# First expert stage: the gates of two prompt tiles added into DRAM by GpSimd's indirect DMAs instead of one-hot products

## The reference

```python
sc, ci = lax.top_k(cand, PEER_TOPK)
eid = (take_along_axis(i1, ci // PEER_TOPK, -1) * N_KEYS + take_along_axis(i2, ci % PEER_TOPK, -1))
gate = jax.nn.softmax(sc, -1)
hid = jax.nn.gelu(einsum('td,thkd->thk', xt, expert_u[eid]))
return einsum('thk,thkd->td', gate * hid, expert_v[eid])
```

## Time and profile before

| | us |
|---|---|
| median of 3 runs | 2101.57 (2098.19 to 2106.11) |
| the profiled execution | 2104.75 |
| its span, first to last instruction | 2103.0 |

### The profile page before, as it was taken

The page is one execution under the profiler, slowest core; times in us unless marked ns, Lnnn a source line. Parts: engine busy times, 40 slices in busy tenths (PEclk is TensorE's granted clock), DMA queues, the critical chain, the costliest instruction groups (busy, mean ns, idle before and its releaser), DMA issues.

```text
span 2103.0 us, 33945 instructions
## 1 busy us (share of the span) xinstructions
PE 2018.1 (96%) x12943; PEld 1851.9 (88%) x12943; DVE 1619.7 (77%) x3030; ACT 794.4 (38%) x1311; POOL 542.5 (26%) x334
## 2 busy tenths in 40 slices
PE   8999889889999899999999999999989999999998
PEld 8998879778866899999999999999978888888886
DVE  6735766565254325999999799999969999999997
ACT  4335453342241322232244344444434333333332
POOL 0000020000000000212111045555537656666530
PEclk9999989989999999999999999999999999999999
DMA  5224210061451402677676579999999999999992
GB/s 172 81 89 129 81 52 1 22 225 41 166 197 62 160 1 89 222 279 247 225 245 237 184 238 334 330 333 333 334 375 396 411 412 411 411 411 411 407 353 93
DMA packets 205520, 483.75 MB, mean 230 GB/s; under 512 B 11983, under 2 KB 104655, under 8 KB 205286
## 3 DMA queue, kind: packets, MB, share of 16 engines
q1 hardware_dynamic: 159334, 314.56, 41.3%
q0 software_dynamic: 46080, 167.79, 21.7%
HBM read 423.29 MB, written 58.36 MB: 229 GB/s over the span
## 4 chain that ended last, share of the span: by engine, by line
PE 58%; DMA 1%; SPq 1%; ACT 0%; DVE 0%; issue 0%; POOL 0%; DVEq 0%
PE ps L3001 24%; PE ps L2609 8%; PE ps L2605 8%; PE ps L2604 8%; PE ps L2595 5%; PE ps L2633 4%; DMA outputs<-peer_v,kept 1%; SPq L2563 0%; SPq L2586 0%; DMA experts<-peer_u 0%; ACT scores L2690 0%; DMA hidden<-kept 0%; PE ps L3027 0%; PE ps L3032 0%; ACT kept L2679 0%
## 5 line engine op out<-in xcount | busy, mean ns | idle before, releaser
L3001 PE MATMUL ps<-v_high_low,gated_high_low 128*128 128x512 f32 x2304 | 526.1, 390 | 8.2 <-ACT gated_high_low L3069 7.4
L3001 PEld LDWEIGHTS ps<-v_high_low,gated_high_low 128*128 128x128 f32 x2304 | 434.0, 189 | 100.1 <-ACT v_high_low L3067 7.7
L2604 PE MATMUL ps<-x_high_low,u_high_low 128*128 128x384 f32 x1024 | 355.6, 347 | 0.2 <-ACT u_high_low L2670 0.2
L2605 PE MATMUL ps<-x_high_low,u_high_low 128*128 128x384 f32 x1024 | 345.0, 337 | 0.0
L3093 POOL DMA_INDIRECT outputs<-peer_v,kept x138 | 255.8, 1854 | 155.7 <-DVE kept L3110 121.5
L2721 POOL DMA_INDIRECT scores<-peer_u,kept x64 | 95.1, 1485 | 733.5 <-DVE kept L2841 556.9
L2679 ACT ACTIVATE kept<-ps 128x384 f32<-128x384 f32 x128 | 62.9, 491 | 407.5 <-PE ps L2609 404.3
L2609 PE MATMUL ps<-x_high_low,u_high_low 128*128 128x384 f32 x1024 | 204.7, 341 | 0.0
L2604 PEld LDWEIGHTS ps<-x_high_low,u_high_low 128*128 128x128 f32 x1024 | 192.5, 188 | 0.5 <-ACT u_high_low L2670 0.5
L2605 PEld LDWEIGHTS ps<-x_high_low,u_high_low 128*128 128x128 f32 x1024 | 192.8, 188 | 0.0
L3110 DVE SCALAR_TENSOR_TENSOR kept<-outputs,kept 128x1024 f32<-128x1024 f32 x136 | 174.3, 1281 | 8.9 <-DMA outputs<-peer_v,kept 5.5
(11 more groups left out here) (471 smaller groups left out, 4136.7 us busy)
## 6 DMA issues: line engine op xcount, KB each, us to landing
experts<-peer_u SPq DMA_DIRECT2D x63, 1024.0 KB
raw_v<-peer_v SPq DMA_DIRECT2D x60, 1024.0 KB
hidden<-kept SPq DMA_DIRECT2D x64, 384.0 KB, 3.5
gates<-scores SPq DMA_DIRECT2D x12, 2048.0 KB
first_hidden<-hidden SPq DMA_DIRECT2D x16, 768.0 KB, 10.4
outputs<-gates SPq DMA_DIRECT2D x16, 768.0 KB
outputs<-hidden SPq DMA_DIRECT2D x16, 768.0 KB
first_gates<-gates SPq DMA_DIRECT2D x15, 768.0 KB
```

Of the source, the lines that this page charges most:

```text
L2604: pe.matmul(o, utr[:, b, HI, k], xr[:, HI, k, 0:DN], start=(k == 0), stop=False)
L2605: pe.matmul(o, utr[:, b, HI, k], xr[:, LO, k, 0:DN], start=False, stop=False)
L3001: ins = pe.matmul(bank(c, 2 * t + h), gr[:, slot, x, DN * b + P * t:DN * b + P * t + P], vr[:, slot, y, D * b + 512 * h:D * b + 512 * h + ...
```

## The change

For tiles 0 and 1 (`SCATTERED`) the gates matrix isn't made by products. Instead:

- POOL sets a tile of 128 x 1024 zeros, ACT waits for it and issues eight DMAs of 2 MB each from it (`ZEROS`), which zero the two thirds of `gates_dram` that belong to tiles 0 and 1. This is the first thing that ACT does in the stage.
- Tile 0 is picked first, then 4, 3, 1, 2. After the picks of tiles 0 and 1 DVE computes the cells of their 128 pairs (`place`, seven small operations), runs as many `low`s as bring it to a given group (`caught_up`), and divides the gates (`divided`), for which ACT has to reach `EXPS_AT`, group 7 for tile 0 and group 31 for tile 1.
- POOL issues 128 accumulating indirect DMAs for each of the two tiles (`scatter`): each adds one number per token, 128 numbers of 4 bytes, into DRAM. After every 16 of them it waits until those before have landed (the 16 pairs of one head have different cells, those of two heads may not).
- The 160 gathers are put between the scatters by fixed counts: none ahead of the 64th scatter of tile 0, 18 by the end of tile 0, 19 more behind it, 96 among the scatters of tile 1, and the last 27 after them.
- Tile 2 keeps the one-hot products: 16 octets in place of 48, in the last 32 steps, four tokens in each; `QT` goes from 2 to 4, `BEFORE` from 39 to 47. Behind the last pick two dots stand after each low (`IN_GAP`).

```diff
-GATES_AT = 25
+EXPS_AT = {0: 7, 1: 31}
-DOTS_BY = {4: 0, GT: 16, 0: 32, 1: 46, 2: 59}
+DOTS_BY = {0: 0, 4: 0, GT: 16, 1: 32, 2: 46}
+ZEROS = 8
+IN_GAP = 2
+GATHERED = [18, 37]
...
+            act.wait_ge(zeros_set, 1)
+            for i in range(ZEROS):
+                g = slice(NG // ZEROS * i, NG // ZEROS * (i + 1))
+                act.dma_start(gates_by_group(c)[:, g, 0:FIRST_G].rearrange("p n g x -> p n (g x)"), over(zeros, 1, [P, NG // ZEROS, FIRST_G * GB * TG])).then_inc(zeroed, 16)
             keep(0, 0)
...
+            def scatter(n, j):
+
+                if j and j % TOPK == 0:
+                    pool.wait_ge(scattered[n], 16 * j)
+                pool.indirect_dma_start(out=gates_flat(c), out_offset=bass.IndirectOffsetOnAxis(ap=cells[n][:, j:j + 1], axis=0),
+                                        in_=gates_of[n][:, j:j + 1], in_offset=None, compute_op=ALU.add).then_inc(scattered[n], 16)
+
+            pool.memset(zeros, 0.0).then_inc(zeros_set, 1)
+            pool.wait_ge(zeroed, 16 * ZEROS)
+            pool.wait_ge(cells_set, 1)
+            for j in range(PAIRS):
+                scatter(0, j)
+                if j >= PAIRS // 2:
+                    gather(GATHERED[0] * (j + 1 - PAIRS // 2) * 2 // PAIRS)
+            gather(GATHERED[1])
+            pool.wait_ge(cells_set, 2)
+            for j in range(PAIRS):
+                scatter(1, j)
+                gather(GATHERED[1] + (PAIRS * 3 // 4) * (j + 1) // PAIRS)
+            gather(ROWSETS)
...
             while lows[0] < UG * BEFORE:
                 low()
+                for _ in range(IN_GAP):
+                    dot()
```

More of the change, by code:

```diff
@@ L71 @@
 K_SEL = _cols(SAMP)
+K_PLACE = _cols(8)
 K_N = _at
@@ L2390 @@
 NTG = DN // TG
+SCATTERED = (0, 1)
+HOTS = [n for n in range(DENSE) if n not in SCATTERED]
+HG = len(HOTS) * (P // TG)
+FIRST_G = NTG - HG
+HC = P * len(HOTS)
 UG = 2
@@ L2487, in phase_hidden @@
     places = words(c, H_B + 512, 2, PAIRS)
-    kept, kt = words(c, H_K, NT, 3, 128), words(c, H_T, 4, DN)
-    gate, inv = words(c, H_V, DN), words(c, H_V + DN, DN)
+    kept, kt = words(c, H_K, NT, 3, 128), words(c, H_T, 4, HC)
+    gate, inv = words(c, H_V, HC), words(c, H_V + HC, HC)
     firm = plain(c.hot[:, :])
     hot2, gated = [firm[:, 0:OCT * P], firm[:, 2 * OCT * P:3 * OCT * P]], [firm[:, OCT * P:2 * OCT * P], words(c, H_HOT, OCT * P)]
+    zeros, cells = firm[:, 0:(NTG - HG) * GB * TG], {n: kept[:, n, 0].bitcast(U32) for n in SCATTERED}
     gst = [words(c, a, NK, TG) for a in F_GST]
@@ L2834, in divided, with place, caught_up @@
                 return v.tensor_tensor(g3, g3, over(head_sum, 2, [P, PH, TOPK]), ALU.mult)
+            def place(n):
+                step(v.tensor_copy(hi, kept[:, n, 0]))
+                step(v.tensor_scalar(hi, hi, 2, None, ALU.logical_shift_right))
+                v.tensor_copy(hif, hi)
+                step(v.scalar_tensor_tensor(lof, kept[:, n, 1], float(NG * NTG * GB), kept[:, n, 0], ALU.mult, ALU.add))
+                step(v.scalar_tensor_tensor(lof, hif, float((NTG - 1) * GB), lof, ALU.mult, ALU.add))
+                step(v.tensor_scalar(lof, lof, float(TG), cst(c, K_PLACE + n, 1), ALU.mult, ALU.add))
+                step(v.tensor_copy(cells[n], lof))
+            def caught_up(q):
+                while lows[0] < UG * q + 1:
+                    low()
+            pick(0, DOTS_BY[0]).then_inc(picked, 1)
+            v.wait_ge(picked, 1)
+            place(0)
+            caught_up(EXPS_AT[0])
+            divided(0, 0).then_inc(cells_set, 1)
             pick(4, DOTS_BY[4]).then_inc(picked, 1)
-            v.wait_ge(picked, 1)
+            v.wait_ge(picked, 2)
             step(v.scalar_tensor_tensor(eid, kept[:, 4, 0], float(NK), kept[:, 4, 1], ALU.mult, ALU.add))
@@ L2844, in _ @@
             pick(GT, DOTS_BY[GT]).then_inc(picked, 1)
-            v.wait_ge(picked, 2)
+            v.wait_ge(picked, 3)
             step(v.scalar_tensor_tensor(tail, kept[:, GT, 0], float(NK), kept[:, GT, 1], ALU.mult, ALU.add))
             v.tensor_copy(ids[:, PAIRS_EACH:], tail).then_inc(ids_set, 1)
-            for n in range(3):
-                pick(n, DOTS_BY[n]).then_inc(picked, 1)
-                v.wait_ge(picked, n + 3)
-                if n == 1:
-                    while lows[0] < UG * GATES_AT + 1 and lows[0] < UG * BEFORE - 1:
-                        low()
-                    step(divided(4, 0))
-                    step(divided(GT, 1))
+            pick(1, DOTS_BY[1]).then_inc(picked, 1)
+            v.wait_ge(picked, 4)
+            place(1)
+            caught_up(EXPS_AT[1])
+            step(divided(4, 1))
+            step(divided(GT, 2))
+            divided(1, 3).then_inc(cells_set, 1)
+            pick(2, DOTS_BY[2]).then_inc(picked, 1)
             while lows[0] < UG * BEFORE:
                 low()
+                for _ in range(IN_GAP):
+                    dot()
             v.wait_ge(sums, 1)
-            step(v.reciprocal(inv, bank(c, 6, DN)))
+            step(v.reciprocal(inv, bank(c, 6, HC)))
             v.tensor_tensor(kt[:, 3], gate, inv, ALU.mult).then_inc(gates_set, 1)
@@ L2863, in _ @@
             low()
-            before, octets = dots[0], NTG * QG // 2 + 3
-            for o in range(NTG * QG // 2):
+            before, octets = dots[0], HG * QG // 2 + 3
+            v.wait_ge(zeroed, 16 * ZEROS)
+            for o in range(HG * QG // 2):
                 t0, slot = OCT * o, o % 2
@@ L2874, in _ @@
                 v.tensor_tensor(k1, k1, over(kt[:, 3, t0:t0 + OCT], 2, [P, OCT, NK]), ALU.mult).then_inc(hot_set, 1)
-                if lows[0] < NK:
-                    low()
+                for _ in range(QT * UG * 2 // QG):
+                    if lows[0] < NK:
+                        low()
                 while dots[0] < min(ROWSETS, before - (before - ROWSETS) * (o + 1) // octets):
```

81 lines of the change are left out of this document (48 added, 33 removed).

## The result

The change makes the kernel slower: 2392.8 us median of 4 runs (2388.2 to 2395.6) against 2100.5 for the kernel before in the same runs. The ratio is 1.1385, 95% interval [1.1354, 1.1415]. The forecast was 2245 us with a range of 2080 to 2400: the place and the kind of the loss were right, its size was half of what came. The profiled execution took 2390.97 us; that is +286 on the 2104.75 of before.

The account below looks back on a forecast made before the run. PE was taken to bound the stage, with DVE in lockstep and nearly full. Saved products -57.6, start +27 and DVE's waits for POOL +44, +44, +87 gave +144 us: 2249 profiled, 2245 us median, range 2080 to 2400.

Parts of the forecast that it names:

- Products, -57.6: One-hot gate products on PE: removing 256 at 0.225 us saves 57.6 us, all of it on the path.
- The start, +27: Stage start: ACT's eight zeroing DMAs fill the queue and delay its first copies and PE by 27 us.
- The scatter's price, 1.24 us: POOL's queue: one scatter takes 1.24 us from start to start, like a gather; bounds 0.30 and 2.28 us.
- 229x - 140.5: Whole change in us, if one scatter costs POOL x us from start to start; turns to a loss at x = 0.61.
- A: DVE's first dot: waits 44 us for the first gathered row behind POOL's scatters.
- B: The fifteen dots after the first: POOL needs 100 us against PE's 56, another 44 us lost.
- C: After the last pick, gap and octets: POOL needs 311 us against PE's 224, 87 us lost.
- The 27 gathers after that are hidden: Stage end: the last 27 gathers take at most 62 us beside PE's last 70, so cost nothing.
- The picks of tile 1 and 2, nothing lost: Picks of tiles 1 and 2: no scatters stand ahead of what they need, so no time is lost.
- Dearer scatters: Rival: scatters cost more than gathers, in POOL or DMA engines; 2.28 us each gives about 2485 us; chance 0.17.
- likeliest case: POOL sets the stage's pace about as worked out, 2180 to 2330 us; chance 0.50.
- Cheap: Rival: scatters cost POOL little, 0.5 us each, making the kernel faster at 2083 or 2059 us; chance 0.15.

Follow-up runs that it names:

- hots-first run: Changed kernel without scatters, zeroing spread, fewer dots left for the end, each octet's two lows behind the one-hots with two dots between: 2087.6 us, 0.9931.
- both tiles, paced: Changed kernel with zeroing spread, lows apart behind the one-hots, dots redistributed, 8 scatters and then 1.8 after each gather: 2319.3 us, 1.1033.

## Why the prediction was right in kind and wrong in size

**Products, -57.6.** Over-sized. With the scatters away and the start mended, 13 us of it became time (hots-first run, 2087.6). "All of it is on the path" is the second step that failed. I had priced it as PE's alone, and left out what PE runs into once its own step is shorter: in the hots-first run's turns the loads of `peer_u` (15.3 us) and DVE's one-hots (10.5 us).

**The start, +27.** Right: 34.28 us of issues, low 1 30 us later, and 30 us back when they are spread. That runs and not bytes fill a queue, at some 2000, fits this row and the two of the earlier trace rows, but no run varied the length of the runs, so it isn't shown.

**The scatter's price, 1.24 us.** This is the first step that failed. I took the gather's row, since both name 128 rows. It is 1.55 + 0.30 = 1.85 us, 0.59 us of it the adding (plain write: 0.96). It lay inside my bounds of 0.30 and 2.28, and I chose the wrong row between them. My formula 229x - 140.5 gives +283 at 1.85; measured +286. That the fit is this close is luck, as the run without scatters shows. Without A, B and C my sum is 2071 us, and it took 2145.7: 75 us too little. The scatters themselves I had at 44 + 44 + 87 = 175 us, and they cost 247: 72 too little, which makes up the rest of the miss of 148. At 1.85 us the formula gives them 314, 67 too much. Two errors of about 70 us cancel in it.

**A, +44** was 84 us (68x - 40.5 at 1.85 gives 85). **B, +44** was 131 - 56 = 75 us (53x - 22 gives 76). Both in their places, dot 1 and the fifteen behind it. **C, +87** was 35 from low 78 to 94 (116.4 for 81) and 99 in the turns (290 for 191), 134 together (108x - 47 gives 153, though it counts only twelve of the 16 octets). Of the 99, 53 are there without any scatters, 21 of which DVE's order gave back in the hots-first run. So with the scatters go only 34 us of the gap (116 against 82) and 46 of the turns (290 against 244), 80 in all: PE's pace, against which I had set POOL's, wasn't to be had there anyway.

**"The 27 gathers after that are hidden"** was wrong: from low 127 to dot 160 it took 31 us, before 13; 17 more. They are 17 in the run without scatters too, and gone in the next (12 us), where fewer of the dots are left for the end; so it wasn't POOL.

**The picks of tile 1 and 2, nothing lost.** Right: low 39 to low 78 is 195 us against 201. **The clock**, left in the range, was granted at 0.54 in the standstill, 0.79 from dot 1 to dot 16 and 0.86 in the turns; no run separates its share. **PE's busy time** was to fall by some 50 us and fell by 5.

**The rivals.** "Dearer scatters" is what happened in part (1.85 us, not 2.28): 2393 us lies above the likeliest case, which ended at 2330. "Cheap" is refuted by the 1.55 us. That one number per row might cost the DMA engines more was not what bound: they were busy 0.22 to 0.79 of the time, and the 14 gathers that DVE waited for behind dot 1 were used 4.2 to 4.9 us after their issue, as the one of before (4.5).

Added up: -57.6 + 30 + 84 + 75 + 134 + 17 = +282, beside the measured +286. Of it 84 + 75 + 80 = 239 go with the scatters by this count, 247 by the run without them.

## What to carry to other kernels

A queue that feeds the critical engine is priced by its total per stretch, each kind of instruction with its own cost from start to start: of the 247 us that the scatters cost, the one other order that was tried alone gave back 69. That their volume holds most of the rest is argued from POOL's full queue, not shown by a run of its own. Half the scatters, 30 of them put where the queue waits anyway and only 16 in the stretch where DVE is full, made a loss of 14% into a gain of 0.6%, together with the zeroing spread and the dots dealt out anew. And work taken off the bounding engine is worth only what the other engines' order and the loads let through, here 13 of 58 us.

## What the runs showed of the hardware that was not expected

- An indirect DMA of 128 numbers costs GpSimd 1.55 us with an addition, 0.96 without, as much as a gather of 128 rows of 4 KB (0.94 to 1.00), and each 0.30 us more to the next. The Trainium skill (DMA: Bandwidth & Descriptors, Anatomy of one DMA) has a fixed cost of about 2.0 us, mostly the receipt; the waits of 2.2 us for a group of 16 scatters (0.3 to 5.1, counted from the end of the last issue) lie near it.
- GpSimd's issues are longer beside DVE's operations with two operands in SBUF (dots and one-hots). In the kernel before, the 60 gathers that hardly any such operation overlaps took 0.94 us (at most 1.11), the 95 that such operations overlap for half their time or more 1.68 to 2.00; in the changed kernel 65 gathers behind 1320 us that hardly any overlaps are at 0.99 in the middle though the DMA engines are at 0.79 in the turns, which speaks against the load of the DMA engines as the reason. The scatters are 1.75 us on the mean over the stage (x256 in 447.0, both tiles paced).
- Eight DMAs of 2 MB in a row hold their issuing engine for 34.28 us; spread, six of them took 0.38 us each and the first two 1.00 together.
- Beside plain small writes every 1.26 us, PE got one matmul in up to 2.8 us (127 us of waits without a visible cause in one run), and DVE and ACT had such waits too, with the DMA engines at 0.11; beside adding ones every 1.85 us PE had none. The cause is open.
